# New start addresses for the buffers of a two-block transformer kernel: the operands of its rounded matmuls are moved to multiples of 1024 bytes

## Time and profile before

| What | Value |
|---|---|
| Time, median of three runs | 1989.58 us (1988.64 to 1992.3) |
| Time of the profiled execution | 1988.22 us |
| Its span, first to last instruction | 1986.2 us |
| TensorE (PE) busy | 1932.0 us, 97% of the span, 16,000 matmuls |
| VectorE (DVE) busy | 1444.0 us, 73% |
| ScalarE (ACT) busy | 1148.4 us, 58% |
| Moved by DMA | 409.84 MB, 206 GB/s on average |

### The profile page before, as it was taken

One profiled execution on the slowest core, in us unless ns is written; L12 is line 12 of the kernel. 1 busy time (PEld: TensorE's weight loads), 2 busy tenths in 40 slices (PEclk: granted clock), 3 DMA queues, 4 the chain that ended last, 5 costly groups with the idle time before them and its releaser, 6 DMA issues.

```text
span 1986.2 us, 37677 instructions
## 1 busy us (share of the span) xinstructions
PE 1932.0 (97%) x16000; PEld 1845.7 (93%) x16000; DVE 1444.0 (73%) x1922; ACT 1148.4 (58%) x1814; POOL 43.3 (2%) x32
## 2 busy tenths in 40 slices
PE   7999999999999999999899999999999999999999
PEld 7898899998989889999899998799999999888999
DVE  5756798888565788988856679766576657986666
ACT  6358846445436875444655566655565556576554
POOL 0100000000010000000001000000000100000000
PEclk9999999999999999999999999999999999999999
DMA  7453377996554346999555543355545554334553
GB/s 276 146 212 107 114 279 307 392 392 255 191 191 149 107 174 235 401 381 385 184 197 197 195 154 126 107 173 191 194 162 212 191 193 167 129 115 162 191 192 128
DMA packets 56182, 409.84 MB, mean 206 GB/s; under 512 B 6608, under 2 KB 6992, under 8 KB 7888
## 3 DMA queue, kind: packets, MB, share of 16 engines
q1 hardware_dynamic: 46512, 330.23, 45.7%
q10 hardware_dynamic: 9504, 77.21, 9.7%
HBM read 406.37 MB, written 1.05 MB: 205 GB/s over the span
## 4 chain that ended last, share of the span: by engine, by line
PE 79%; DVE 14%; ACT 5%; issue 2%; DMA 0%; DVEq 0%; ACTq 0%; SPq 0%
PE bank L603 25%; PE bank L604 24%; PE bank L605 24%; DVE weights_low L405 4%; ACT weights_high L383 1%; DVE work L2440 1%; DVE scratch L1464 1%; DVE work L1536 1%; ACT work L465 1%; PE bank L954 1%; DVE work L566 1%; DVE h_low L572 1%; ACT weights_high L384 0%; DVE work L1626 0%; DVE scratch L1621 0%
## 5 line engine op out<-in xcount | busy, mean ns | idle before, releaser
L405 DVE TENSOR_TENSOR weights_low<-raw_weights,weights_high 128x1024 fp32r<-128x1024 f32 x608 | 728.3, 1237 | 344.4 <-ACT weights_high L383 339.9
L603 PE MATMUL bank<-h_high,weights_high 128*128 128x256 f32 x3024 | 853.4, 282 | 14.6 <-DVE h_low L572 11.2
L604 PE MATMUL bank<-h_low,weights_high 128*128 128x256 f32 x3024 | 841.0, 278 | 0.0
L605 PE MATMUL bank<-h_high,weights_low 128*128 128x256 f32 x3024 | 841.0, 278 | 0.0
L383 ACT ACTIVATE weights_high<-raw_weights 128x1024 fp32r<-128x1024 f32 x296 | 313.4, 1059 | 601.0 <-PE bank L605 570.2
L603 PEld LDWEIGHTS bank<-h_high,weights_high 128*128 128x128 f32 x3024 | 568.3, 188 | 31.3 <-issue 13.9
L604 PEld LDWEIGHTS bank<-h_low,weights_high 128*128 128x128 f32 x3024 | 568.5, 188 | 0.6 <-issue 0.5
L605 PEld LDWEIGHTS bank<-h_high,weights_low 128*128 128x128 f32 x3024 | 568.2, 188 | 0.0
L603 PE MATMUL bank<-weights_high,hidden_high 128*128 128x256 f32 x1280 | 358.0, 280 | 6.9 <-DVE work L2514 2.8
L604 PE MATMUL bank<-weights_low,hidden_high 128*128 128x256 f32 x1280 | 355.8, 278 | 0.0
L605 PE MATMUL bank<-weights_high,hidden_low 128*128 128x256 f32 x1280 | 355.7, 278 | 0.0
(11 more groups left out here) (304 smaller groups left out, 1870.1 us busy)
## 6 DMA issues: line engine op xcount, KB each, us to landing
raw_weights<-in_stream SPq DMA_DIRECT2D x310, 1024.0 KB, 4.8
work<-in_ada ACTq DMA_DIRECT2D x64, 1152.0 KB, 9.4
consts<-in_consts SPq DMA_DIRECT2D x1, 2048.0 KB, 12.8
work<-in_row ACTq DMA_DIRECT2D x2, 836.0 KB, 5.5
x<-in_x SPq DMA_DIRECT2D x1, 1024.0 KB, 4.8
out_x<-x SPq DMA_DIRECT2D x4, 256.0 KB, 2.2
gain_row<-in_final SPq DMA_DIRECT2D x1, 512.0 KB, 13.4
vec<-in_vec SPq DMA_DIRECT2D x1, 169.0 KB, 12.7
```

The costliest lines, as they stand in the source:

```text
L405: dve.tensor_tensor(low[:, c], raw[:, c], high[:, c].bitcast(F32), ALU.subtract).then_inc(m.raw_done[plan.index[name] % RAW], 1)
L603: pe.matmul(out, aH, bH, start=start, stop=False, skip_group_check=True)
L604: pe.matmul(out, aH, bL, start=False, stop=False, skip_group_check=True)
L605: return pe.matmul(out, aL, bH, start=False, stop=stop, skip_group_check=True)
```

## The change

The order of the allocations is changed and one unused buffer of 896 bytes is put first. No instruction is added, removed or moved; only the addresses in the instructions differ.

```diff
+        self.start = sb("start", 224)
         self.raw = sb("raw_weights", RAW * CH)
         self.wH = sb("weights_high", 2 * CH, F32R)
         self.wL = sb("weights_low", 2 * CH, F32R)
-        self.x = sb("x", 2 * D)
-        self.gain_row = sb("gain_row", D)
-        self.mask_r = sb("mask_rounded", 5 * P, F32R)
-        self.fox_r = sb("fox_rounded", 16, F32R)
         self.hH = sb("h_high", KT * T, F32R)
         self.hL = sb("h_low", KT * T, F32R)
         self.uH = sb("hidden_high", 2 * 512, F32R)
         self.uL = sb("hidden_low", 2 * 512, F32R)
+        self.x = sb("x", 2 * D)
+        self.gain_row = sb("gain_row", D)
+        self.mask_r = sb("mask_rounded", 5 * P, F32R)
         self.scratch = sb("scratch", 3072)
         self.work = sb("work", 18432)
         self.consts = sb("consts", NC)
         self.trig = sb("trig", 4 * T)
+        self.fox_r = sb("fox_rounded", 16, F32R)
         self.vec1 = sb("vec1", 2 * NV1)
```

## The result

The changed kernel takes 2042.03 us (median of 4 runs, 2040.34 to 2042.4) against 1989.52 us: ratio 1.026, 95% interval 1.0242 to 1.0278. It is slower by 52.5 us, outside the range of the prediction, and slower than if every rounded product had taken the long pitch (1989.6 + 29.4 = 2019 us).

What follows compares the result with a forecast made beforehand. TensorE's rounded products times their pitch were taken to bound the kernel. From the profiled execution, 1988.2 - 10 (products) - 0.2 (DMA) = 1978.0 us; the median lies 1.4 us above, so 1979.5 us, range 1958 to 2012.

Steps and rivals of the forecast that it cites:

- the long pitch: Start-to-start distance of neighbouring rounded products on TensorE, 116 to 120 ns (mean 117.8); the short one is 112 to 115 ns.
- What bounds the kernel: TensorE, busy 97% of the span: time is nearly the number of rounded products times their pitch, 1646.5 us or 83%.
- the changes of pitch at the orientation switch: Pitch changed at 121 of 124 pauseless switches from activations to weights moving; with one offset class these should go.
- The rival that addresses decide nothing: Something else than addresses chooses TensorE's pitch; time stays 1989.6, within 4 us; chance 26%.
- The bounds of the rounded products: TensorE's matmuls: all long +29.4 us, all short -33.8 us, at the transposes' pitch 87 us less; taken 11.9 us less.
- The moving operand's alignment decides the preference: On TensorE, moving operands at multiples of 128 prefer the short pitch, raising its share from 47% to 66%: 11.9 us less.
- The slower rival: Without pitch changes at switches, the long pitch lasts through block 2's feed-forward steps: +23.4 us, time 2011.5; chance 30%.
- VectorE, ScalarE: The splits on both engines keep 1237 and 1059 ns within 1%; taken as 0, bounds -1 to +1 us.
- DMA: Shifted destinations of raw_weights and work; only the load of x on the path; taken as -0.2 us.
- N: Experiment theory, TensorE: a moving read collides with the load of the next matmul's stationary operand, giving some 120 ns.
- P: Experiment theory, TensorE: differences to the next load of 192, 64, 192 in a triple give short pitch; 64, 192, 64 long.
- J: Experiment theory, TensorE: a moving operand whose offset jumps between matmuls gets the long pitch, one whose offset stays the short.

Runs made afterwards that it cites:

- e2: Changed kernel with 64 bytes put between weights_low and h_high, so h and hidden lie 64 past a multiple of 1024, weights at 0; 1997.89 us, ratio 1.0022.
- e12: Changed kernel with offsets modulo 256: weights high 0, low 128; h and hidden high 64, low 192; 2028.4 us, ratio 1.0171.
- e1: Changed kernel with its unused 896-byte first buffer moved behind hidden_low; weights, h and hidden start 128 past a multiple of 1024; 2041.09 us, ratio 1.0236.
- e10: Original kernel with the 64-byte fox_rounded moved from ahead of h_high to behind hidden_low; 2040.68 us, ratio 1.0232.
- e11: Changed kernel with offsets modulo 256: weights high and low 0; h and hidden high 64, low 192; 1998.61 us, ratio 1.0019.
- e13: Changed kernel with offsets modulo 256: weights 0; h high 192, low 64; hidden high 64, low 192; 2001.69 us, ratio 1.0064.
- e15: Changed kernel with offsets modulo 256: weights high 64, low 192; h and hidden 0; 1985.42 us, ratio 0.9978.
- e14: Changed kernel with offsets modulo 256: weights high 0, low 128; h and hidden all 64; 2014.84 us, ratio 1.0131.

## Why the prediction was wrong

- *What bounds the kernel.* Right: the time is the number of rounded products times their pitch. Of 54 us more span the pitch explains 59, with some 5 given back, mostly in waits.
- *Addresses have a part in it; the changes of pitch at the orientation switch come from the offsets.* Right in kind. After the change these switches have no effect (one pitch), and with 64 bytes between the operands they are back at the same places (e2). The rival that addresses decide nothing is out.
- *The bounds of the rounded products.* This is the step that failed, and the term of the sum is that of the rounded products: put at -11.9 us (10 of them to be had), it measured +59 us (14,280 x 4.16 ns). I wrote that all products at the long pitch, +29.4 us, bound the cost above. But 118 ns was the worst of the offsets in the trace, whose two operands always lie 64 apart (modulo 128), not the worst there is. The kernel after has a difference of 0, which no stream of before had, and its pitch is a third one, 120 ns. A bound for a state that the trace doesn't show was taken from the states that it does show. Nor is 120 ns the worst: e12 has a mean of 120.6 ns with weights moving.
- *"Neither a new heap below nor one above is seen there."* The trace did hold a hint. In the single products at a change of orientation the moving operand and the next stationary one have like offsets. I saw that they take 113 to 120 ns and read it as nothing new. In fact, of the 118 with weights in both places (moving weights, then stationary ones) 55 take exactly 120 ns, well over half of all the distances of that value in the trace (89 of 14,282), and all 55 stand behind a product at the long pitch. It was no more than a hint: the other 63 take 113 to 119 ns, and of the 124 with activations in both places, at like offsets too, none takes 120 ns (113 to 118). Why the two kinds differ is open.
- *The moving operand's alignment decides the preference.* Wrong, and with it the sign of the forecast. e1 moves all operands together and nothing changes; e2 leaves the weights and gains everything back. It is the difference, modulo 256, and with a gap of 192 in place of 64 the preferences change places while the moving weights stay at offset 0. The 99 of 110 against 25 of 38 runs after a pause were a real difference, but the orientations differ in the sign of the difference just as well as in the moving operand's offset, and I took the one reading without weighing the other.
- *The slower rival* named the right sign, but its mechanism (the long state lasts) and its price (2011.5 us; its own terms give 1989.6 + 23.4 - 1 = 2012.0) were those of the same too narrow bound. The low end of the range has a slip of the same size: it takes 32 us off, where the working has 33.8 (1955.8 us). Neither decides anything.
- *VectorE, ScalarE.* Taken as 0 and right: 1236, 1057 and 1044 ns against 1237, 1059 and 1044.
- *DMA.* Taken as -0.2 us, and nothing was gained: `raw_weights` lands after 4.8 us before and after, `work` after 9.4 and 9.6, and the load of x after 4.8 and 5.0. One piece in 33 fewer, if the rule for a start at a multiple of 256 bytes (the Trainium skill, "DMA: Bandwidth & Descriptors", How a descriptor splits into AXI transactions) held for the destination, does not show in this trace. That a faster TensorE would wait for its loads in block 1, for which the forecast gave up 1.9 us, was not tested, since TensorE became slower.
- *What the Trainium skill says of TensorE.* That TensorE has two independent SBUF reads and never waits on anyone (the Trainium skill, "SBUF — State Buffer", Who interferes with whom) was read in the prediction as saying that addresses cost nothing. That reading is refuted: by the operands' offsets alone the same instructions take 119.9 ns on average in place of 115.8, some 52 us of this kernel. Whether it is the two reads that wait on each other, no run measured. The isolated pitch of N/2.4 + 2.5 ns (the Trainium skill, "TensorE: Matmul & The Clock Gate", Back-to-back issue gap), by which 109 ns is the estimate here, was reached by no rounded product of these 17 kernels: no distance from one to the next is below 112 ns. With 113.4 and 117.8 ns it is exceeded by 4 and by nearly 9 ns.
- *The chances.* 30% for slower, with the range ending at 2012. The range was made of mechanisms that I could price, and left nothing for a stream that the trace had never shown.

## What to carry to other kernels

Where TensorE is the bound and float32r matmuls of 256 columns, each with its own stationary load, follow each other, compare the SBUF offsets of the moving and the stationary operands modulo 256 bytes. Equal offsets cost some 3% of the pitch against a difference of 64 (119.9 ns against 116.7 in e2 and 115.8 before), and a small buffer put in or taken out between the two operands' buffers is enough to get there. One ahead of both moves them alike and changes nothing (e1). Starting all operands at multiples of 256 bytes or more gives equal offsets: it is the trap, not the cure. When a change creates a combination that the trace does not contain, look for single instructions that have it, count how often each duration occurs among them, and don't take the worst of the known states for a bound.

## What the runs showed of the hardware that was not expected

- The pitch of float32r matmuls of 256 columns, each with its own stationary load of 128 columns, takes separate values at a granted clock of 0.998 of 2.4 GHz: 113.4 and 117.8 ns at differences of 64 and 192, and 120.0 ns at equal offsets, at which 13,533 of 14,273 distances are the same to the nanosecond. Other differences spread (with 128: 112 to 128 ns, mean 118.7). Transposes of 128 columns with an operand in `consts` and one in `x` are not touched: the difference of these two buffers changed by 64 bytes, and 26 distances from start to start average 108.7 ns before and 108.8 ns after.
- At differences of 64 and 192 the pitch is one of two, and the one found lasts until a pause or until the offsets change; the same code took one in the first layer and the other in the second (33.69 and 32.44 us). If which one it is differs between executions too, that would explain the spread of the kernel before, 1985.9 to 2001.0 us and 1985.9 to 2006.0 us on two chips, beside which the kernels at 120 ns stay within 1.7 us (e1, four runs) and 0.9 us (e10, four runs). It was not shown, since only one execution of each kernel was profiled. What decides it is open: e11, e13 and e15 are near all short in one orientation, and theories N, P and J each failed (N on e12, P on e13, J on e14).
- That two SBUF reads of TensorE collide is the reading which fits the period of 256 bytes and the dependence on the difference, and the 120 ns need no other engine at work; no run measured the reads themselves.
